# A two-layer S5/pool trunk on one core: both layers written out, the feed-forward in eight chunks, layer 1's tables made during layer 0

## The chip, the cores and the metric

One core of a Trainium2 chip runs one launch of the kernel. The metric is the device time of that launch in microseconds (us), the median over several runs. TensorE (PE) multiplies, VectorE (DVE), ScalarE (ACT) and GpSimd (POOL) do the elementwise work, and SyncE (SP) issues DMAs, as ACT and POOL also can. Each engine executes its own list of instructions in order and waits on semaphores.

## The reference

1088 frames (1024 of a prompt, 64 of a running stream) of 1024 channels pass two layers and a last RMSNorm. All of it is float32.

```python
# per layer
hn = rmsnorm(x, g_mix);  u_a, u_b = split(hn @ w_in)          # 1024 -> 512 + 512
lam_dt = lam * exp(log_dt);  lam_bar = exp(lam_dt)             # 32 groups x 64 complex states
b_bar = ((lam_bar - 1) / lam) * b
h_t = lam_bar * h_{t-1} + b_bar u_a_t                          # scan over the frames
y = Re(C h) + d * u_a;  z = gelu(y);  y_a = z * sigmoid(z @ w_glu)
y_b = (trailing means over 2/4/8/16 frames - u_b) @ w_pool * scale
x = x + concat(y_a, y_b) @ w_out
x = x + square(relu(rmsnorm(x, g_ffn) @ w_ff1)) @ w_ff2        # 1024 -> 4096 -> 1024
# returned: y of both streams, the last states, the last 15 rows of u_b, per layer
```

## The kernel before, in words

Activations lie with channels on the partitions, all 1088 frames along the free axis. A product of float32 accuracy is three fast products: each operand is split into a high part (rounded) and a low part (the rest), and high x high, low x high, high x low add up in PSUM. A **tile** is 128 output channels by 1088 frames in one of two PSUM buffers (`tile0`, `tile1`), written by 9 matmuls per 128 input channels (three products by three column chunks of 408, 408 and 272): 72 matmuls with 1024 input channels ("K=8" below), 36 with 512 ("K=4"). Weights come in **blocks** of 512 KB, one for each K=8 tile or two K=4 tiles: SP fetches block b into `w_raw` when the block two before it has been split, ACT makes `w_high` (L590), DVE makes `w_low` (L778). Two slots of each alternate.

A layer has 96 tiles. In order: 8 tiles of w_in (WIN, K=8), 4 small pool tiles (L494), 8 tiles of the w_out half for y_b ("wob", K=4), 4 of w_glu (K=4), 8 of the w_out half for y_a ("woa", K=4), and the feed-forward, 4 chunks of 1024 hidden channels, each with 8 tiles of w_ff1 (FF1, K=8) and 8 of w_ff2 (FF2, K=8).

The SSM is blocked by 8 frames (136 blocks J). Four quarters q of 8 groups each pass:

- tables from the parameters (`angles` L825, `discretised` L850, both DVE), rotations by doubling (`double` L308; groups halves on DVE and on POOL), `drive_weights(q)` L898 on DVE, `carry_weights(q)` L1198 on POOL; on PE, `prep(q)` L430 transposes the drive weights (L437) and multiplies out the intra-block kernels (L449), ACT stores those to DRAM;
- `drives(q)` on PE (L463) and ACT, then a rotation of the drives (`rotate` L290, `early_pre` L944, `pre` L939), a scan (L963) and a rotation back (`post` L974). DVE does these for some quarters, POOL does others (L1238 to L1253);
- `carry(q)` on PE (L511): intra-block and carried part into the small PSUM buffers, `output(q)` L1072 on DVE adds d*u, ACT stores the rows to DRAM (`store` L698), SP reads them back as y_a, ACT takes the GELU (L712) and splits (L714).

Since `x` shares its memory with `u_b` and the pool's buffers, x is kept in DRAM (L620, L600) and read back (L379) when the pool tiles are done; that, the carry weights (L370) and the intra-block kernels (L375) go through SP's queue in that order at block B_WOB+3. The order of work on each engine is written out by hand; the PE list interleaves the small products between WIN tiles (L469 to L485) and the carries between wob tiles (L534 to L542). Both layers are one body in a loop over l (L337, L427, L624, L807, L1178); the middle chunks of the feed-forward are loops too.

The hidden activation (`hidden` L1117): DVE takes relu times the inverse root from PSUM (L1121), squares it (L1124), splits the next weight block (L778), and makes the hidden low part (L1128); ACT makes the hidden high part (L736). FF2's tile waits before each 128 hidden channels for `hid_made` (L554 to L556) in the first tile of a chunk.

```python
def ff2(c, m, odd):
    ff_tile(odd, 16 * c + 8 + m, ghi, glo,
            None if odd else lambda k: pe.wait_ge(hid_made, l * 32 + 8 * c + k + 1))
```

RMSNorm: ACT squares x tile by tile (`finish` L592), POOL adds the squares (L1171), PE sums over the partitions (L423), ACT takes the root (L606), DVE inverts (L790).

## Time and profile before

| what | us |
| --- | --- |
| median of three runs (2304.25 to 2305.23) | 2305.21 |
| span of the profiled execution, first to last instruction | 2305.6 |
| PE busy in it | 2182.5 (95%) |
| DVE busy | 1085.5 (47%) |
| ACT busy | 422.5 (18%) |
| POOL busy | 305.1 (13%) |

The profile gives for the execution its span and the busy time in it; nothing outside the span is listed, and the span stands 0.4 us above the median of the runs. The share of an engine says little by itself here: the two feed-forwards (about 400 to 1150 us and 1520 to 2275 us) have PE busy without a break, and the stretches between them, one mixer per layer, do not. The prediction therefore reads the execution by stretches.

### The profile page before, as it was taken

What the parts mean: (1) busy time and instruction counts of PE and PEld (TensorE: products, weight loads), DVE (VectorE), ACT (ScalarE), POOL (GpSimd) and SP (SyncE); (2) the same over time, 40 slices, a digit from 0 to 9 for tenths busy, and PEclk for the clock granted to TensorE, in tenths of its full rate; (3) what the DMA queues carried; (4) which work ended last, traced back from release to release, by engine and by line L of the source; (5) the groups of instructions that cost most, each with busy time, mean ns of one, the idle gap of its engine ahead of it and who ended that gap; (6) DMA issues with size and microseconds to landing.
All of it is one profiled execution on the core that took longest, in us unless ns stands there. A gap on an engine that the chain in (4) does not pass through costs nothing.

```text
span 2305.6 us, 32257 instructions
## 1 busy us (share of the span) xinstructions
PE 2182.5 (95%) x12894; PEld 2125.5 (92%) x12894; DVE 1085.5 (47%) x1448; ACT 422.5 (18%) x462; POOL 305.1 (13%) x372
## 2 busy tenths in 40 slices
PE   6896999999999999999998979999999999999995
PEld 5785799999999999999997868999999999999995
DVE  7999445532332242233379973554224224323435
ACT  3111043210110111111221202421011101101121
POOL 4637003000000000000235630110000000000011
PEclk8998799999999999999998978999999999999998
DMA  5618221111111111111225633111111111111123
GB/s 214 135 50 170 54 71 37 46 46 45 46 45 37 45 45 45 36 45 65 95 91 113 108 112 77 37 47 46 45 37 45 45 45 40 45 42 45 45 86 125
DMA packets 72121, 153.04 MB, mean 66 GB/s; under 512 B 6752, under 2 KB 40848, under 8 KB 71776
## 3 DMA queue, kind: packets, MB, share of 16 engines
q1 hardware_dynamic: 46384, 117.79, 18.2%
q10 hardware_dynamic: 24992, 31.60, 4.3%
q0 software_dynamic: 656, 2.48, 0.3%
q8 instruction: 54, 0.88, 0.2%
q14 instruction: 35, 0.29, 0.0%
HBM read 119.96 MB, written 31.88 MB: 66 GB/s over the span
## 4 chain that ended last, share of the span: by engine, by line
PE 78%; DVE 15%; issue 5%; ACT 1%; DMA 0%; DVEq 0%; POOL 0%; ACTq 0%; SPq 0%; POOLq 0%
PE tile L405 74%; DVE drive_products L815 2%; PE small L528 1%; PE small L527 1%; DVE drive L969 1%; DVE rotations L321 1%; DVE h_low L783 1%; DVE drive L967 1%; DVE w_low L778 1%; PE small L529 1%; DVE pool_s L815 1%; DVE x L1063 1%; DVE dve_products L319 1%; DVE work_s L803 1%; DVE ub L933 1%
## 5 line engine op out<-in xcount | busy, mean ns | idle before, releaser
L405 PE MATMUL tile<-h_high,w_high 128*128 128x408 f32 (+1 forms) x1920 | 432.0, 333 | 27.8 <-DVE h_low L783 23.9
L405 PE MATMUL tile<-h_low,w_high 128*128 128x408 f32 (+1 forms) x1920 | 427.1, 331 | 0.0
L405 PE MATMUL tile<-h_high,w_low 128*128 128x408 f32 (+1 forms) x1920 | 426.8, 331 | 0.0
L1063 DVE TENSOR_TENSOR x<-tile,x 128x816 f32<-128x816 f32 (+1 forms) x192 | 129.9, 717 | 551.9 <-PE tile L405 551.9
L405 PEld LDWEIGHTS tile<-h_high,w_high 128*128 128x128 f32 x1920 | 324.3, 190 | 35.6 <-DVE h_low L783 26.6
L405 PE MATMUL tile<-hidden_high,w_high 128*128 128x408 f32 (+1 forms) x1536 | 338.4, 328 | 0.0
L405 PE MATMUL tile<-hidden_low,w_high 128*128 128x408 f32 (+1 forms) x1536 | 338.4, 328 | 0.0
L405 PE MATMUL tile<-hidden_high,w_low 128*128 128x408 f32 (+1 forms) x1536 | 338.4, 328 | 0.0
L405 PEld LDWEIGHTS tile<-h_low,w_high 128*128 128x128 f32 x1920 | 324.1, 190 | 0.2
L405 PEld LDWEIGHTS tile<-h_high,w_low 128*128 128x128 f32 x1920 | 324.0, 190 | 0.2
L590 ACT ACTIVATE w_high<-w_raw 128x1024 fp32r<-128x1024 f32 x166 | 174.4, 1051 | 784.7 <-PE tile L405 784.2
L778 DVE TENSOR_TENSOR w_low<-w_raw,w_high 128x1024 fp32r<-128x1024 f32 x166 | 217.5, 1310 | 146.0 <-ACT w_high L590 146.0
L1171 POOL TENSOR_TENSOR rms<-rms,work_s 128x1088 f32<-128x1088 f32 x20 | 54.7, 2733 | 1674.7 <-ACT work_s L597 1660.2
L1121 DVE SCALAR_TENSOR_TENSOR work_r<-tile,rms 128x816 f32<-128x816 f32 (+1 forms) x128 | 86.7, 719 | 380.4 <-PE tile L405 380.2
L405 PEld LDWEIGHTS tile<-hidden_high,w_high 128*128 128x128 f32 x1536 | 256.5, 188 | 0.0
L405 PEld LDWEIGHTS tile<-hidden_low,w_high 128*128 128x128 f32 x1536 | 256.5, 188 | 0.0
L405 PEld LDWEIGHTS tile<-hidden_high,w_low 128*128 128x128 f32 x1536 | 256.5, 188 | 0.0
L736 ACT ACTIVATE hidden_high<-work_r 128x1088 f32 (+1 forms) x64 | 71.5, 1117 | 626.8 <-DVE work_r L1121 626.8
L1124 DVE TENSOR_TENSOR work_s<-work_r 128x1088 f32<-128x1088 f32 x64 | 82.7, 1292 | 2.2
L1128 DVE TENSOR_TENSOR hidden_low<-work_s,hidden_high 128x1088 f32 (+1 forms) x64 | 82.2, 1285 | 0.0
L405 PE MATMUL tile<-y_b_high,w_high 128*128 128x408 f32 (+1 forms) x192 | 49.1, 369 | 31.7 <-DVE x L1063 31.4
L405 PEld LDWEIGHTS tile<-y_b_high,w_high 128*128 128x128 f32 x192 | 36.3, 213 | 33.9 <-DVE x L1063 32.5
(174 smaller groups left out, 1844.7 us busy)
## 6 DMA issues: line engine op xcount, KB each, us to landing
w_raw<-w_blocks SPq DMA_DIRECT2D x166, 512.0 KB, 3.5
x_kept<-x ACTq DMA_DIRECT2D x24, 544.0 KB, 2.7
x<-x_kept SPq DMA_DIRECT2D x16, 544.0 KB, 13.6
x<-x_t ACTq DMA_DIRECT2D x8, 544.0 KB, 10.4
ua_dram<-u_a SPq DMA_DIRECT2D x8, 544.0 KB, 7.4
u_blocks<-ua_dram SPq DMA_DIRECT2D x32, 136.0 KB, 6.5
ya_dram<-u_blocks ACTq DMA_DIRECT2D x64, 68.0 KB, 2.2
y_a<-ya_dram SPq DMA_DIRECT2D x8, 544.0 KB, 3.4
```

The costliest lines, as they stand in the source:

```text
L319: step(tensor_tensor(t1, w_, fi, ALU.mult))
L321: step(tensor_tensor(rot[:, ri, :, n:2 * n], t0, t1, op))
L405: last = pe.matmul(ps[tile][:, c, 0:(b - a) * J], lhs, xt[:, k, a * J:b * J], start=(k == order[0] and n == 0), stop=(k == order[-1] and n ...
L590: act.activation(whi[:, s, :], raw[:, s, :], ACT.Copy).then_inc(whi_made, 1)
L736: act.activation(out, tr[:, :], ACT.Square).then_inc(ghi_made, 1)
L778: v.tensor_tensor(wlo[:, s, :], raw[:, s, :], f32(whi[:, s, :]), ALU.subtract).then_inc(wlo_made, 1)
L815: step(v.tensor_tensor(out, a, b, op))
L1063: ins = v.tensor_tensor(xt, pt_, xt, ALU.add)
L1121: ins = v.scalar_tensor_tensor(out, pt_, 0.0, r, ALU.max, ALU.mult)
L1124: v.tensor_tensor(ts[:, :], tr[:, :], tr[:, :], ALU.mult).then_inc(sq_v, 1)
L1128: v.tensor_tensor(lo, ts[:, :], f32(hi), ALU.subtract).then_inc(hid_made, 1)
L1171: pool.tensor_tensor(rms[:, :], rms[:, :], (tr, ts)[m % 2][:, :], ALU.add).then_inc(sq_added, 1)
```

## The change

- The loop over layers and the loops in the feed-forward are gone; every instruction is written out, with the layer as a constant.
- The feed-forward has 8 chunks (NC) of 512 hidden channels: 4 tiles of w_ff1 with K=8, then 8 tiles of w_ff2 with K=4, in the order m = 0..7, k = 0..3. Weight blocks stay at 64 per layer; an FF2 block holds two tiles and is read from two blocks of the old layout.
- The tables of layer 1 (angles, discretisation, rotations, drive weights, carry weights, kernels) are made on DVE, PE and ACT inside layer 0's feed-forward: the first four pieces after the four hidden tiles of chunk 0, the quarters in chunks 1 to 4. POOL's queue stores them to DRAM, and in chunk 6 SP reads rotations and drive weights back.
- All work on the states is DVE's: rotations, carry weights, pre, scan, post. POOL keeps the sums of squares and issues DMAs. The final states are copied out of the rotated ones instead of being computed by POOL.
- d*u goes into the intra-block kernel (`fix_kernel`, DVE), and ACT instead of DVE takes the carry's result out of PSUM (`carried`).
- Layer 0's angles and discretisation are placed among the loads of x at the very start; rotations follow before the first inverse root. x of layer 0 is read back from the input, not from a kept copy.
- The carries lie elsewhere among the wob tiles, and otherwise in each layer.

```diff
+            def turned(q, sign, shift, tmp):
+                ...
+                tt(t[0], cos, re, ALU.mult)
+                tt(t[1], sin, im, ALU.mult)
+                tt(t[2], cos, im, ALU.mult)
+                tt(t[3], sin, re, ALU.mult)
+                step.wait()
+                tt(to_re, t[0], t[1], ALU.add if sign < 0 else ALU.subtract)
+                tt(to_im, t[2], t[3], ALU.subtract if sign < 0 else ALU.add)
...
 @block.sync
+                    if b == B_WOB + 2:
                         sp.wait_ge(tile_done, LT + KD)
                         sp.wait_ge(cy_out, 128 * (l + 1))
+                        sp.dma_start(cy[:, :, :, :], cy_dram[l]).then_inc(cy_in, 16)
                         sp.wait_ge(k_out, 128 * (l + 1))
...
+                            sp.dma_start(kin[CH * tau:CH * tau + CH, :, :],
+                                         k_dram[l, :, :, a:a + P]).then_inc(kin_in, 16)
                         sp.wait_ge(tile_free, LT + T_POOL + KA + 2)
+                        for m in range(6):
+                            sp.dma_start(x[:, m, :], (x_in, x_hist)[l][m]).then_inc(x_back[m], 16)
...
 @block.tensor
+                    if l == 0:
+                        if 3 <= t < 7:
+                            drives(0, t - 3)
+                        if 2 <= t < 6:
+                            turns(0, t - 2)
+                        if t >= 4:
+                            kernels(0, t - 4)
+                    elif 2 <= t < 6:
+                        drives(1, t - 2)
...
+                if l == 0:
+                    for n in range(4):
+                        wob(n)
+                    carry(0)
+                    carry(1)
+                    wob(4)
+                    carry(2)
+                    wob(5)
+                    carry(3)
+                    wob(6)
+                    wob(7)
+                else:
+                    wob(0)
+                    carry(0)
+                    wob(1)
+                    carry(1)
+                    wob(2)
+                    wob(3)
+                    carry(2)
+                    wob(4)
+                    carry(3)
+                    for n in range(5, 8):
+                        wob(n)
...
+                for cc in range(NC):
+                    for m in range(KA):
+                        ...
+                        product(n % 2, m % 2, 0, KD, hhi, hlo, ready)
+                        ...
+                        if l == 0 and m == 2 and cc in PREP_CHUNKS:
+                            turns(1, PREP_CHUNKS[cc])
+                    n = ff2_tile(l, cc, 0)
+                    for m in range(KD):
+                        ...
+                        product((n + m) % 2, m // 2 % 2, KA * (m % 2), KA, ghi, glo, None if m else
+                                lambda k: pe.wait_ge(hid_made, (l * NC + cc) * KA + k + 1))
+                        if l == 0 and m == 3 and cc in PREP_CHUNKS:
+                            kernels(1, PREP_CHUNKS[cc])
...
 @block.vector
+                if m == 1:
+                    angles(0)
+                if m == 4:
+                    discretised(0)
+            split_lo(1)
+            rotations(0, 0)
...
+                if l == 0:
+                    inverse(0)
+                    win_a(0)
+                    rotations(0, 1)
+                    rotations(0, 2)
+                    win_a(1)
+                    rotations(0, 3)
+                    drive_weights(0, 0)
+                    win_a(2)
+                    drive_weights(0, 1)
+                    carry_weights(0, 0)
+                    win_a(3)
+                    ...
+                    pooled(0, 0)
+                    v.wait_ge(lp_in, 16)
+                    for i in range(KA):
+                        y_b(i)
+                    fix_kernel(0, 3)
+                    post(0, 0)
+                    post(0, 1)
+                    wob(0)
+                    pre(0, 2, late)
+                    scan(0, 2)
+                    ...
...
+                        if l == 0:
+                            if cc == 0:
+                                (angles, discretised, lambda l: rotations(l, 0), lambda l: rotations(l, 1))[m](1)
+                            elif cc in PREP_CHUNKS:
+                                q = PREP_CHUNKS[cc]
+                                if m == 0 and q == 0:
+                                    rotations(1, 2)
+                                    rotations(1, 3)
+                                if m == 1:
+                                    drive_weights(1, q)
+                                if m == 3:
+                                    carry_weights(1, q)
...
 @block.gpsimd
+            for q in range(4):
+                carry_weights_out(0, q)
+                if q:
+                    kernels_out(0, q - 1)
+            kernels_out(0, 3)
+            states_out(0)
+            add_squares(1)
+            rotations_out()
```

PREP_CHUNKS maps the chunks 1 to 4 to the quarters 0 to 3. `drive_weights(1, 0)` waits for the store of the rotations (`rot_out`), because its products overlay them.

## Rows read from the trace of the kernel before

**Rows 1.** The page: the chain that ended last, share of the span by engine.

```profile
PE 78%; DVE 15%; issue 5%; ACT 1%; DMA 0%; DVEq 0%; POOL 0%; ACTq 0%; SPq 0%; POOLq 0%
```

**Rows 2.** Busy time by stretch: length, PE, PEld, DVE, ACT, POOL, clock, DMA, GB/s.

```profile
43.00:180.00 137.00, 124.57 (x822) 114.20 (x822) 126.20 (x243) 30.11 (x52) 61.87 (x91) 0.93 0.40 97
180.00:244.00 64.00, 43.71 (x228) 40.44 (x228) 62.77 (x120) 5.62 (x8) 36.71 (x54) 0.87 0.70 144
400.00:1150.00 750.00, 750.00 (x4501) 749.92 (x4500) 256.21 (x263) 114.09 (x110) 15.29 (x6) 1.00 0.15 49
1166.00:1301.00 135.00, 122.89 (x824) 113.28 (x823) 125.09 (x240) 29.59 (x51) 60.52 (x83) 0.94 0.37 86
1301.00:1366.00 65.00, 47.52 (x234) 43.49 (x234) 63.60 (x121) 6.12 (x9) 37.52 (x57) 0.82 0.67 151
```

**Rows 3.** The chain in order of time: start, length, what.

```profile
305.41 1.36 DVE x L1063 x2
...
400.90 753.00 PE tile L405 x4518
...
1154.97 13.77 PE tile L405 x81
...
1426.59 1.35 DVE x L1063 x2
```

**Rows 4.** Timeline of DVE and ACT around one FF1-to-FF2 step: start, length, instruction.

```profile
481.95 1.36 DVE L1121 SCALAR_TENSOR_TENSOR work_r<-tile,rms 128x816 f32<-128x816 f32 x2 [6.09 <-PE tile L405]
...
486.58 1.28 DVE L1128 TENSOR_TENSOR hidden_low<-work_s,hidden_high 128x1088 fp32r<-128x1088 f32 x1
```

**Rows 5.** Timeline of PE: prep(0) up to the next tile, and prep(1) after its wait.

```profile
82.82 1.03 PE L437 MATMUL small<-prep_in,x_quarter 128*128 128x128 f32 x8
87.86 0.77 PE L405 MATMUL tile<-h_high,w_high 128*128 128x408 f32 x3
...
113.12 0.58 PE L449 MATMUL small<-y_quarter,bbar_re 64*16 64x128 f32 x2 [9.10 <-POOL y_quarter L1216]
```

**Rows 6.** Timeline of DVE: drive weights, a doubling, a rotation, with and without POOL beside.

```profile
86.27 0.68 DVE L815 TENSOR_TENSOR drive_products<-power_re,bbar_re 128x512 f32<-128x512 f32 x1
...
90.38 0.24 DVE L1027 COPY rotations<-phasor 128x4 f32<-128x4 f32 x2
...
91.64 0.17 DVE L318 TENSOR_TENSOR drive_products<-rotations 128x8 f32<-128x8 f32 x1
...
194.20 1.40 DVE L321 TENSOR_TENSOR rotations<-dve_products 128x128 f32<-128x128 f32 x1
...
210.00 0.71 DVE L299 TENSOR_TENSOR dve_products<-rotations,drive 128x544 f32<-128x544 f32 x1
...
214.19 1.35 DVE L1063 TENSOR_TENSOR x<-tile,x 128x816 f32<-128x816 f32 x2
```

**Rows 7.** The DMA queue of SP around the end of WIN in layer 0: start, length of issue.

```profile
176.56 0.33 SPq L370 DMA_DIRECT2D carry_weights<-cy_dram  x1
177.00 16.88 SPq L375 DMA_DIRECT2D intra_weights<-k_dram  x8
194.15 8.33 SPq L379 DMA_DIRECT2D x<-x_kept  x8
```

**Rows 8.** Busy time in stretches of 4 us, columns as in rows 2.

```profile
188.00:192.00 4.00, 3.73 (x22) 3.73 (x23) 3.90 (x9) 1.27 (x2) 3.52 (x6) 1.00 1.28 95
208.00:212.00 4.00, 1.86 (x6) 1.82 (x7) 3.97 (x7) 0.00 (x0) 0.84 (x4) 0.50 1.02 410
248.00:252.00 4.00, 4.00 (x13) 3.00 (x14) 0.71 (x3) 0.00 (x0) 1.18 (x4) 0.50 0.03 10
280.00:284.00 4.00, 4.00 (x24) 3.03 (x23) 1.24 (x4) 0.00 (x0) 0.00 (x0) 1.00 0.00 0
```

**Rows 9.** DMA issues on the page: size of each, median us from issue to landing.

```profile
k_dram<-k_stage ACTq DMA_DIRECT2D x16, 32.0 KB, 1.6
...
k_dram<-zeros POOLq DMA_DIRECT2D x1, 224.0 KB, 8.1
```

More of the change, by code:

```diff
@@ L394, in _, with products @@
         @block.tensor
         def _(pe):
-            def product(tile, slot, half, n_k, xh, xl, ready=None, order=range(KD)):
-                order = order[:n_k]
+            def products(tile, slot, col, k, xh, xl, first, last):
+                for n, (wt, xt) in enumerate(((whi, xh), (whi, xl), (wlo, xh))):
+                    lhs = wt[:, slot, col * P:(col + 1) * P]
+                    for c, (a, b) in enumerate(CHUNKS):
+                        mm = pe.matmul(ps[tile][:, c, 0:(b - a) * J], lhs, xt[:, k, a * J:b * J],
+                                       start=(first and n == 0), stop=(last and n == 2))
+                return mm
@@ L399, in product @@
+            def product(tile, slot, col0, n_k, xh, xl, ready=None, backwards=False):
+                order = list(range(n_k))[::-1] if backwards else list(range(n_k))
                 for k in order:
@@ new lines, in kernels @@
+            def kernels(l, q):
+                d = prep_of[l]
+                pe.wait_ge(y_quart, l * 4 + q + 1)
+                for gl in range(2):
+                    out = small_at(SM["kernel", l, q, gl])
+                    rows = slice(ST * gl, ST * gl + ST)
+                    for g in range(4):
+                        for ri, b in enumerate((d.bbr, d.bbi)):
+                            mm = pe.matmul(out[0:CH, g * P:(g + 1) * P], b[rows, 4 * q + g, :],
+                                           d.yq[rows, ri, g, 0:BLK, :].rearrange("p t c -> p (t c)"),
+                                           start=(ri == 0), stop=(ri == 1))
+                    mm.then_inc(small_done, 1)
@@ new lines, in drives @@
+            def drives(l, q):
+                pe.wait_ge(ublk_in[q], 16 * BLK * (l + 1))
+                if l == 0:
+                    pe.wait_ge(small_free, SM["turn", 0, q, 1] + 1 + 2)
+                elif q == 0:
+                    pe.wait_ge(bt_in, 16)
+                for g in range(4):
+                    n = SM["drive", l, 4 * q + g]
+                    out = small_at(n)
+                    bt = stage0[:, g] if l == 0 else bt_all[:, 4 * q + g]
+                    for gl in range(2):
+                        for ri in range(2):
+                            mm = pe.matmul(out[ST * gl:ST * gl + ST, ri * J:(ri + 1) * J],
+                                           bt[:, ri, ST * gl:ST * gl + ST],
+                                           ublk[:, 2 * (4 * q + g) + gl, :], start=True, stop=True)
+                    mm.then_inc(small_done, 1)
@@ L469, in _ @@
+            pe.wait_ge(ones_set, 1)
+            for l in range(LAYERS):
+                LB, LT = l * NB, l * NT
                 for t in range(KD):
@@ L607, in roots, with turns @@
                                    scale=1.0 / DM, bias=eps_col[:, :]).then_inc(small_free, 1)
+            def turns(l, q):
+                d = prep_of[l]
+                if l == 0 and q:
+                    act.wait_ge(small_done, SM["drive", 0, 4 * q - 1] + 1)
+                if l:
+                    if q == 0:
+                        act.wait_ge(rot_out, 16)
+                    else:
+                        act.wait_ge(bt_out, 16 * q)
+                for ri in range(2):
+                    n = SM["turn", l, q, ri]
+                    act.wait_ge(small_done, n + 1)
+                    act.activation(d.bt[:, :, ri, :], sm[n % 2][:, :].rearrange("p (g n) -> p g n", n=P),
+                                   ACT.Copy).then_inc(small_free, 1)
@@ new lines, in kernels @@
+            def kernels(l, q):
+                d = prep_of[l]
+                if l * 4 + q:
+                    act.wait_ge(k_out, 32 * (l * 4 + q))
+                if l == 0 and q == 0:
+                    act.wait_ge(ua_out, 16 * KA)
+                for gl in range(2):
+                    n = SM["kernel", l, q, gl]
+                    act.wait_ge(small_done, n + 1)
+                    act.activation(d.kst[:, gl, :, :], sm[n % 2][0:CH, :].rearrange("p (g n) -> p g n", n=P),
+                                   ACT.Copy).then_inc(small_free, 1)
```

1484 lines of the change are left out of this document (753 added, 731 removed).

## The prediction

> **What bounds the kernel now.** I read the page's chain first: 78% PE, 15% DVE [rows 1]. As a share this only says that PE is nearly the bound everywhere, so I went on to the busy time by stretch [rows 2]. In 400 to 1150 us PE is busy 750.00 of 750.00 at clock 1.00: the feed-forward is purely PE's, one matmul each 753.00/4518 = 0.1667 us [rows 3], so a K=8 tile (72) takes 12.0 us and a K=4 tile (36) 6.0. DVE is busy a third of it, so there is room beside PE, and nothing to win for PE. In the mixers it is the other way round. From 43 to 180 DVE is busy 126.20 of 137, from 180 to 244 62.77 of 64 while PE has 43.71; layer 1 repeats this (125.09 of 135, 63.60 of 65) [rows 2]. PE's idle time and its low clock there are what can be won. Layer 1's WIN starts at 1154.97 and the last wob tile is added at 1426.59, so this mixer takes 271.6 us [rows 3].
>
> I take the change in four stretches and measure each against the profiled execution (span 2305.6; the runs' median is 0.4 below, so the sum is made on 2305 without correction).
>
> **Feed-forward, both layers: +14 each.** The matmul count is the same. What changes is when FF2's first tile needs the last hidden part. After an FF1 tile, DVE starts at 481.95 and finishes the low part at 486.58 + 1.28 = 487.86, 5.9 us later [rows 4]. Before, that part was k=7 of a K=8 tile, needed 7 x 1.5 = 10.5 us into it: hidden. Now it is k=3 of a K=4 tile, needed 4.5 us in. With 0.2 us for the end of the last matmul and 0.1 for the wait, PE stands 5.9 + 0.3 - 4.5 = 1.7 us, in each of 16 chunks: 27 us, half of it per layer. Nothing covers it, as the k and m orders are plain and the two PSUM tiles leave PE nothing else in its list. Bounds: 1.4 (no overheads) to 2.5 a chunk, 22 to 40. The doubled number of adds to x (1.35 us each [rows 6]) is hidden: DVE has 6 us a tile. The weight reads keep a cadence of 12 us a block.
>
> **Tables in layer 0's feed-forward: +35.** PE's part: transposes and kernels of a quarter took 82.82 to 87.86 with one wait of 0.85 in between, so 4.2 us [rows 5]; four make +17, on the path because PE has no gap there. DVE's part is hidden where a piece fits behind a hidden tile (12 - 5.9 = 6.1 us): drive weights take 90.38 - 86.27 = 4.1, carry weights (576 for 512 elements) 4.6 [rows 6]. It doesn't fit in two places. A doubling of few elements costs about 1.0 us (copies and first one 90.38 to 91.64), one of 512 about 4.1; in between I scale: rotations piece 0 (8 doublings, 240 elements in all) 9.5 us, piece 1 (4, 768) 8.7, pieces 2 and 3 4.4 each [rows 6]. Chunk 0: DVE is already late by the inverse root; angles (3.5) and discretised (6) use the slack up, and piece 0 stands ahead of the last hidden part. Walking DVE's list gives 9 us of wait in FF2's first tile instead of 1.7, then 2 more because piece 1 stands ahead of the first add: +10. After a wait of 9.10 before, the kernels of prep(1) ran slow [rows 5]; a wait of this length costs about 4 more in low clock. Chunk 1: pieces 2 and 3 (8.8), then the 2.2 MB store of the rotations, must be done before drive weights 0, which PE's transposes wait for in order. At the 410 GB/s of one row the store takes 5.4 us, at 95 GB/s 23 [rows 8]; its rows are 17 KB long, so I take 7.5 with issue, and get +4 (bounds 0 to 20). Together 17 + 14 + 4 = +35 (17 to 55). The read back in chunk 6 (4.3 MB, 11 us at 410 GB/s) fits into the 19 us that a block is fetched ahead.
>
> **Layer 1's mixer: -52.** Without tables, DVE has in it 7 (inverse) + 9.6 (four u_a) + 4 x 4.2 (pre) + 4 x 3.7 (scan) + 4 x 5 (post) + 12 (u_b) + 21 (pool sums) + 6 (y_b) + 14 (wob) = 121 us (where no group shows a duration of this kind, it is read from the same timeline of DVE as rows 6), and PE becomes the bound. PE's walk from WIN's start: tiles 96 and three sums 2, drives after four of them 11, so WIN ends at 109; pool tiles and their ACT-DVE relay to 122; wob 0 at 128. Then the new wait: the carries now stand right behind wob 0, and they need the intra-block kernels. These are read after WIN, in SP's queue behind the carry weights. Before, the issue ran from 176.56 to 193.9 and then x [rows 7], with 95 GB/s at 1.28 of the DMA engines' share at 188 and 410 GB/s from 208 on, when x came [rows 8]: the kernels land some 28 us after the end of WIN. Before, five wob tiles stood ahead and hid this. Now 109 + 28 = 137, so PE waits 9 us, and carry 0 may run at the low clock. A carry (4 of 16 pairs) takes 8.7 us at clock 1.00 and twice the matmul time at 0.50: 24 matmuls in 4 us against 13 [rows 8]. With it slow (16), wob 1 partly slow (8), three carries 26 and six wob tiles 36: 137 + 16 + 8 + 26 + 36 = 223 against 271.6, -49; with all at full speed 208, -64. I take -52.
>
> **Layer 0's head and mixer: +9.** Added to DVE: angles and discretised stand in the head, where DVE was already busy throughout: 9.3 us later (they leave the mixer). Then rotations in pieces, 27 us, all on DVE; carry weights 4 x 4.6 = 18 come from POOL, as do half the pre and post. Taken off: the lock between the two. Beside POOL's products a DVE product of 128 elements took 1.40 us, while one of 544 took 0.71 when alone [rows 6]; POOL's 61.87 and 36.71 us [rows 2] go. With clean durations DVE's list from the split of block 1 (52 us) to the last post sums to 178 us, before waits: 230. The waits, by walking the four lists: PE's first transposes wait for drive weights 0 until 95 us, and the WIN tile behind them is late for u_a (5); carry weights 2 for a small product (3); y_b for ACT, which holds each kernel until the store before it has landed, 4 us through POOL's queue, between 1.6 and 8.1 [rows 9] (9); and the largest, the first wob add waits for x. The last kernel is fixed only behind y_b, at 204, is stored by 208, the kernels' read takes 20 more and x comes after it: 231 us against 214 when DVE is there (17). So DVE's last post ends near 264, where PE has passed wob 3 at 248. From there carries 35 and four wob tiles 24 make 307 at full clock, 323 with two carries and a wob tile slow as before, against 305.41 [rows 3]: +1 to +18, with an error of my walk of about 10 either way. I take +9.
>
> A rule that speaks against the change: the last kernel's store goes through POOL's queue now, and the rows there are 8.1 us for the one store by POOL on the page against 1.6 for the same matrix from ACT [rows 9]; I take 4. By the Trainium skill (SBUF — State Buffer, "SBUF: two separate sides") a DMA issued on GpSimd has its descriptors written by that engine, which a two-port VectorE operation locks out, 620 ns alone against about 3100 beside a copy. By it this store would come about 2.5 us later than alone, and layer 0's mixer would be longer by as much; no row here shows it.
>
> The loops' turns cost nothing now: 0.1667 us a matmul hold across all of them [rows 3]. The Trainium skill (Runtime: NRT & Kernel Launch, "Instruction fetch mechanics") has a taken branch out of the sequential window stall the fetch, so that unrolling would gain; by that rule the sum would be lower, by the rows it is not.
>
> **Sum.** 14 + 14 + 35 - 52 + 9 = +20, so 2305 + 20 = 2325 us.
>
> **Rivals.** (A) My forecast: 2325, own range 2308 to 2342. Chance 0.50. (B) Faster: DVE relieved of POOL walks ahead of PE in layer 0 as well, and the clock stays up through the carries since ACT drains PSUM at once. Then layer 0's mixer gains 12, layer 1's 64, and the feed-forward costs 27 + 28 = 55: -21, 2284. For it: DVE stands at 98% from 180 to 244 in both layers beside a busy POOL [rows 2], and a full-clock carry is seen at 280. Against it: the same carries ran at 0.50 at 248 [rows 8], and the x wait of layer 0 is a matter of order. It decides from the point where layer 0's first wob add comes before 220 us. Chance 0.28. (C) The chunk stalls are worse: waits of 9 us in chunks 0 and 1 leave PE at the low clock, the rotations' store takes the long bound, and layer 0's x comes late: 27 + 55 - 45 + 15 = +52, 2357. For it: the store shares queues with the weights. Against it: the feed-forward's DMA share is 0.15 [rows 2]. Chance 0.14. (D) The gains and costs cancel: 2305, chance 0.08, the middle between A and B.
>
> **How the numbers follow.** About 0.2% (5 us) is what a measurement tells from no change. Faster by more: B and a little of A's and D's edge, 0.30. Within: 0.08. Slower: 0.62. The range that leaves out 2 in 10 goes from 2282 (just below B) to 2350 (most of A, the near half of C).
>
> **What would show it.** The time between FF1's last tile and the fourth k of FF2 in the profile after: a wait of PE on hidden_low of 1.5 to 2 us, sixteen times. PE busy in the feed-forward of layer 0 below full, with one wait near 9 us in its first chunk. Layer 1 from WIN's start to the last wob add near 220 us, with PE waiting for a DMA before its first carry. Layer 0's last wob add between 300 and 325 us, and DVE waiting some 15 us for x. The prediction is wrong if the feed-forwards run without gaps, since then the sum is -7, or if layer 1's mixer stays above 240.

## The result: 0.3% slower, 2310.6 us where 2325 was forecast

| | median of the runs | profiled run | its span |
|---|---|---|---|
| before | 2305.14 us (20 runs) | about 2307 | 2305.6 |
| after | 2310.55 us (20 runs, 2305.72 to 2319.65) | 2317.74 | 2315.9 |

The ratio is 1.0033, 95% interval 1.0022 to 1.0044. The direction was right, the move was +5.4 us and not +20. The time of the kernel before's profiled run isn't on record; in all of its runs that have both, the time is 1.5 to 1.6 us above the span, hence about 2307. So this execution was some 2 us slower than its kernel's median, and that of the changed kernel 7.2.

The stretches first, in the profiled executions. The marks are those of [rows 3]: PE's start of layer 1's WIN and the start of each layer's last wob add. WIN starts before the last part of x is complete: the last FF2 add ends 0.3 us after that mark in the kernel before and 6.1 after it in the changed one.

| stretch | forecast | before | after | difference |
|---|---|---|---|---|
| start to layer 0's last wob add | +9 | 305.4 | 314.4 | +9.0 |
| to layer 1's WIN | +49 | 849.6 | 887.2 | +37.6 |
| to layer 1's last wob add | -52 | 271.6 | 225.9 | -45.7 |
| to the end | +14 | 879.0 | 888.4 | +9.4 |
| sum | +20 | | | +10.3 |

Busy time of the changed kernel by stretch, columns as in [rows 2]:

```profile
43.00:180.00 137.00, 117.56 (x776) 109.39 (x776) 123.24 (x252) 23.60 (x41) 15.09 (x15) 0.92 0.28 83
180.00:244.00 64.00, 41.84 (x199) 36.47 (x198) 34.16 (x88) 8.20 (x12) 2.06 (x4) 0.73 0.64 130
400.00:1150.00 750.00, 728.26 (x4427) 719.38 (x4426) 342.08 (x483) 109.78 (x117) 14.32 (x22) 0.99 0.17 57
1155.00:1290.00 135.00, 130.41 (x847) 125.93 (x846) 88.99 (x142) 36.51 (x47) 17.83 (x7) 1.00 0.34 109
1290.00:1355.00 65.00, 52.60 (x259) 45.77 (x258) 44.89 (x107) 8.58 (x13) 0.00 (x0) 0.84 0.71 141
```

In layer 1's first mixer stretch DVE falls from 125 busy us to 89: the tables are gone from it. The feed-forward, full before, now leaves PE idle for 21.7 of 750 us. In layer 0 DVE is busy only 34 of 64 us from 180 on. Four of PE's waits (total, times, longest) say for what; the largest total, for `h_low`, was 23.9 us before. The 13.6 us more all stand ahead of 50 us, in the head where the angles and the discretisation went, for the 9.3 that were forecast there:

```profile
PE tile L427 <- DVE h_low L865: 37.5, 9, 12.0
PE tile L427 <- DVE hidden_low L1324: 31.5, 16, 8.5
PE tile L427 <- DVE x L1200: 18.3, 2, 18.1
PE small L463 <- DVE x_quarter L1012: 12.1, 2, 9.7
PE small L566 <- issue: 8.7, 1, 8.7
```

The last four in time order, from the timelines of DVE and PE (the bracket is the idle time ahead):

```profile
234.06 1.35 DVE L1200 TENSOR_TENSOR x<-tile,x 128x816 f32<-128x816 f32 x2 [17.96 <-DMA x<-x_t]
...
456.01 1.28 PE L427 MATMUL tile<-hidden_high,w_high 128*128 128x408 f32 x3 [8.46 <-DVE hidden_low L1324]
...
539.82 1.09 PE L463 MATMUL small<-prep_in,x_quarter 128*128 128x128 f32 x8 [2.38 <-DVE x_quarter L1012]
...
1342.16 0.79 PE L566 MATMUL small<-u_blocks,intra_weights 128*128 128x136 f32 x2 [8.74 <-issue]
```

They are the waits of the forecast, near its sizes: 17, 9, 4 and 9 us had been walked out. The chain through layer 1's feed-forward shows the small one, one turn per chunk of 97.16 us:

```profile
1558.97 1.29 DVE L1319 TENSOR_TENSOR work_s<-work_r 128x1088 f32<-128x1088 f32 x1
1562.21 1.28 DVE L1324 TENSOR_TENSOR hidden_low<-work_s,hidden_high 128x1088 fp32r<-128x1088 f32 x1
...
1563.55 91.18 PE tile L427 x549
```

After 1563.55 the next restart is at 1660.71. Of the 31.5 us that PE waits for `hidden_low` the first chunk has 8.46, so it stands 1.53 us in each of the other 15. The row also has what I had not expected: 91.18 / 549 = 0.1661 us a matmul, where it was 753.00 / 4518 = 0.1667 [rows 3].

### The profile page after: what moved, and what is told of

Its sections match the earlier page's. It is cut to its first block and busy times, and to the rows that moved or that the text cites. A ratio compares the mean times of both kernels' runs of the same rounds, so it can differ in the third digit from the quotient of the medians.

```text
span 2315.9 us, 29009 instructions
## 1 busy us (share of the span) xinstructions
PE 2160.1 (93%) x12894; PEld 2098.9 (91%) x12894; DVE 1120.3 (48%) x1622; ACT 423.4 (18%) x483; POOL 120.4 (5%) x80
## 3 DMA queue, kind: packets, MB, share of 16 engines
q10 hardware_dynamic: 12960, 17.96, 2.5%
## 5 line engine op out<-in xcount | busy, mean ns | idle before, releaser
L1200 DVE TENSOR_TENSOR x<-tile,x 128x816 f32<-128x816 f32 x320 | 216.6, 718 | 580.6 <-PE tile L427 552.8
L427 PE MATMUL tile<-hidden_high,w_high 128*128 128x408 f32 (+1 forms) x1536 | 340.6, 330 | 31.6 <-DVE hidden_low L1324 31.5
L860 DVE TENSOR_TENSOR w_low<-w_raw,w_high 128x1024 fp32r<-128x1024 f32 x164 | 210.4, 1283 | 101.3 <-ACT w_high L635 101.3
L815 ACT ACTIVATE hidden_high<-work_r 128x1088 fp32r<-128x1088 f32 x64 | 71.4, 1116 | 645.7 <-DVE work_r L1316 645.7
L1324 DVE TENSOR_TENSOR hidden_low<-work_s,hidden_high 128x1088 fp32r<-128x1088 f32 x64 | 82.2, 1284 | 0.0
L865 DVE SCALAR_TENSOR_TENSOR h_low<-x,layer_params,h_high 128x1088 fp32r<-128x1088 f32 x24 | 43.9, 1830 | 27.3 <-ACT h_high L650 27.3
## 6 DMA issues: line engine op xcount, KB each, us to landing
x<-x_t SPq DMA_DIRECT2D x8, 544.0 KB, 13.3
x<-x_kept SPq DMA_DIRECT2D x8, 544.0 KB, 13.3
```

Source lines behind the costliest of these rows:

```text
L427: mm = pe.matmul(ps[tile][:, c, 0:(b - a) * J], lhs, xt[:, k, a * J:b * J], start=(first and n == 0), stop=(last and n == 2))
L815: act.activation(ghi[:, m, :], tr[:, :], ACT.Square).then_inc(ghi_made, 1)
L860: v.tensor_tensor(wlo[:, b % 2, :], raw[:, b % 2, :], f32(whi[:, b % 2, :]), ALU.subtract).then_inc(wlo_made, 1)
L865: v.scalar_tensor_tensor(hlo[:, m, :], x[:, m, :], gain[:, m:m + 1], f32(hhi[:, m, :]), ALU.mult, ALU.subtract).then_inc(h_made, 1)
L1200: ins = v.tensor_tensor(xt, pt_, xt, ALU.add)
L1324: v.tensor_tensor(glo[:, m, :], ts[:, :], f32(ghi[:, m, :]), ALU.subtract).then_inc(hid_made, 1)
```

## The experiments

All were timed in turns with the kernel before; medians in us. The ratios come from the comparison with its runs in turn and are not the quotients of two medians. The stretches in the table are of the profiled executions: to the end of layer 0's last wob add; from the end of the last WOA add to that of the last FF2 add (FF 0, FF 1); and between FF 0 and layer 1's last wob add (mixer 1).

| kernel | median | ratio, 95% | mixer 0 | FF 0 | mixer 1 | FF 1 |
|---|---|---|---|---|---|---|
| before | 2305.1 | | 306.8 | 767.3 | 272.6 | 767.3 |
| after | 2310.6 | 1.0033 | 315.8 | 810.2 | 221.1 | 776.6 |
| e1_order | 2295.6 | 0.9948 (0.9934, 0.9962) | 312.4 | 806.9 | 221.0 | 764.4 |
| e2_place | 2302.5 | 0.9995 (0.9982, 1.0008) | 310.9 | 801.2 | 220.3 | 776.4 |
| e3_xfirst | 2312.9 | 1.0034 (1.0022, 1.0046) | 314.3 | 809.9 | 220.9 | 776.4 |
| e4_l1wob | 2306.2 | 1.0012 (0.9998, 1.0025) | 315.5 | 812.0 | 219.3 | 776.5 |
| e5_petables | 2298.6 | 0.9966 (0.9953, 0.9979) | 313.7 | 796.9 | 220.1 | 776.5 |
| e7_spaced | 2299.0 | 0.9981 (0.9960, 1.0003) | 312.1 | 810.4 | 211.5 | 776.5 |
| b1_unroll | 2305.5 | 0.9993 (0.9982, 1.0005) | 307.3 | 767.3 | 272.2 | 767.3 |
| b2_layers | 2295.0 | 0.9952 (0.9926, 0.9978) | 306.4 | 767.2 | 272.8 | 767.2 |
| b3_shift | 2339.7 | 1.0136 (1.0090, 1.0182) | 328.9 | 762.3 | 298.1 | 763.9 |
| c1_all | 2272.9 | 0.9849 (0.9834, 0.9864) | 314.9 | 792.2 | 220.3 | 764.4 |
| c2_spaced | 2261.3 | 0.9828 (0.9793, 0.9862) | 304.4 | 794.0 | 204.6 | 764.4 |

A profiled execution is one of its kernel's runs. Most lie within 3 us of the median, but those of the changed kernel (7.2 us above), e4 (11.3, the slowest of 11), c1 (10.5, the slowest of 5) and b2 (10.2) do not, and b3's lies 6.2 above. Mixer 0 is the same work in the changed kernel, e1, e2, e4, e5 and e7, and reads 310.9 to 315.8 us: less than 5 us there is no effect.

**e1_order: is the wait per chunk a matter of FF2's order?**

```diff
-                    for m in range(KD):
+                    for m, ks in ((0, (0, 1, 2)), (1, (0, 1, 2)), (0, (3,)), (1, (3,))):
+                        ...
+                    for m in range(2, KD):
```

> The changed kernel with FF2's first two tiles of every chunk interleaved on PE: tile 0 with k = 0 to 2, tile 1 with k = 0 to 2, then tile 0's k = 3 and tile 1's k = 3; all else as in the changed kernel. My theory (the wait of 1.53 us on the last hidden part is a matter of how much of FF2 stands ahead of it, 4.5 us against the 5.9 that ACT and DVE need): with 9 us of matmuls ahead of it the wait goes in all 15 plain chunks, 15 x 1.5 = 23 us, and that of 8.5 us in the first chunk shrinks by 4.5; layer 1's and layer 0's mixers are unchanged: 23 to 27 us below the changed kernel's 2310.6, about 2285. Rival 1 (FF2 becomes bound by what comes later, since tile 0 ends later, both tiles end within 1.5 us of each other and the adds of tile 0 and 1 then lag, so that FF2's third tile waits for a free PSUM tile): half of it or nothing comes back, 2298 to 2310, with a wait of PE on tile_free's side in place of the one on hidden_low. Rival 2 (PE's wait is recorded time in which the engine would have paid a weight load or a fetch anyway): 2310.

Layer 1's feed-forward went from 776.6 to 764.4: 12.2 us, 8 x 1.53, and the waits are gone. So the cause of this term is shown. Layer 0's gave only 3.3 more. Five of its chunks gained 1.5 each. The first became 2.4 us longer (107.9 for 105.5), for PE waits there twice, first for DVE's drain of the fourth hidden tile and then for the late adds. The second gained nothing: behind the wait for the drive weights the clock was at 0.50 from 538.0 to 541.4. The last became 1.6 us longer, for PE waits for the adds there too (third row), and 1.15 us more ahead of WIN:

```profile
446.74 1.27 PE L427 MATMUL tile<-hidden_high,w_high 128*128 128x408 f32 x3 [3.91 <-DVE work_r L1326]
460.95 1.25 PE L427 MATMUL tile<-hidden_high,w_high 128*128 128x408 f32 x3 [3.82 <-DVE x L1210]
...
1180.13 0.73 PE L427 MATMUL tile<-hidden_high,w_high 128*128 128x408 f32 x3 [1.25 <-DVE x L1210]
```

The first chunk, where DVE has rotations in its list, shows rival 1. In all it gained 15 us for the 23 to 27 expected.

**e2_place: is the first chunk's wait DVE's rotations?**

```diff
-                (angles, discretised, lambda l: rotations(l, 0), lambda l: rotations(l, 1))[m](1)
+                if m < 2:
+                    (angles, discretised)[m](1)
...
+        if l == 0 and cc == 0 and m < 7:
+            ...
+            for n2, h2 in (((1, 0), (1, 1)), ((2, 0), (2, 1)), ...)[m]:
+                doubled(1, n2, h2)
```

> The changed kernel with pieces 0 and 1 of layer 1's rotations moved: they no longer stand behind hidden tiles 2 and 3 of the first chunk, but, two doublings at a time, behind the adds of FF2 tiles 0 to 6 of that chunk. My theory (the wait of 8.5 us in the first chunk is VectorE's list, with 9.5 us of rotations ahead of the last hidden part, and the low clock behind it follows from the wait): the wait falls to the 1.5 us of the other chunks, and the clock stays at 1.00: 7 us from the wait and 2 to 3 from the clock, about 10 us below the changed kernel, 2300. Rival 1 (the doublings behind the adds make the adds late, and FF2's tiles then wait for a free PSUM tile): 1 to 2 us come back at each of 3 or 4 tiles, 2305. Rival 2 (the wait comes from the inverse root and the hidden tiles themselves, not from the tables): unchanged, 2310.

```profile
442.81 0.77 PE L427 MATMUL tile<-hidden_high,w_high 128*128 128x408 f32 x3 [1.53 <-DVE hidden_low L1324]
```

The first chunk takes 96.4 us for 105.5, the median is 8.1 us lower, and the three matmuls behind the wait take 0.77 us, not 1.28: at the end of the long wait the clock had been at 0.50. So 6.9 us of the 9.1 are the wait and the rest is clock. My theory held, and no wait for a free PSUM tile took the place of the old one.

**e5_petables: what do the tables cost PE?**

```diff
-                    for g in range(4):
+                    for g in range(4 if l == 0 else 1):
```

> The changed kernel with PE's share of layer 1's tables cut to a quarter: of each quarter's 8 transposes 2 and of its 16 small products 4 are done, the rest is left out (so that three quarters of layer 1's kernels and drive weights aren't computed); the waits and all of VectorE's and ScalarE's work stay. My theory (the tables' matmuls are added to PE's list, 4.2 us a quarter at full clock, 17 in all, because PE has no gap in the feed-forward): 3/4 of 17 less, 13 us, and layer 0's feed-forward 797 us instead of 810; the kernel 2298. Rival (these small matmuls cost next to nothing, and what the tables cost PE is the waiting for VectorE, which stays): within 3 us of the changed kernel, 2308 to 2311.

Layer 0's feed-forward was 13.3 us shorter. In the changed kernel a chunk with tables takes 101.40 us and one without 97.16, so a quarter costs 4.24; with a quarter of the matmuls 98.13. That is linear in PE's work, and 4 x 4.24 = 17.0 stands beside the forecast's 17.

**e3_xfirst: is the 18 us wait for x a matter of SP's queue?**

```diff
+                    if l == 0 and b == B_WOB + 2:
+                        sp.wait_ge(tile_free, LT + T_POOL + KA + 2)
+                        for m in range(6):
+                            sp.dma_start(x[:, m, :], x_in[m]).then_inc(x_back[m], 16)
```

> The changed kernel where, in layer 0 alone, SyncE issues the reads of x tiles 0 to 5 ahead of those of the carry weights and of the kernels, and not behind them. My theory (the 18 us that VectorE and PE stand before layer 0's first wob add are the order of SyncE's queue: x waits behind the kernels' read, which waits for the last kernel's store): the wait goes, but PE then meets the carries, which need the kernels that now come some 4 us later, after seven wob tiles: layer 0's last wob add comes 8 to 16 us earlier, 2297 to 2302. Rival 1 (the kernels are what everything waits for, and the 18 us reappear in front of the first carry): less than 3 us, 2308 to 2311. Rival 2 (the reads of x, started early, collide with the drive weights' and kernels' stores and make WIN's last tiles late): slower than 2311.

The first wob add came at 210.6 instead of 234.1, and then PE met the kernels:

```profile
212.10 0.73 PE L432 MATMUL tile<-y_b_high,w_high 128*128 128x408 f32 x3 [1.20 <-DVE x L1205]
220.95 0.76 PE L432 MATMUL tile<-y_b_high,w_high 128*128 128x408 f32 x3 [2.65 <-DVE x L1205]
238.31 0.79 PE L571 MATMUL small<-u_blocks,intra_weights 128*128 128x136 f32 x2 [9.59 <-issue]
```

The wait was one of 18 and is now three of 13.4 together, the largest ahead of the first carry, as rival 1 has it. Mixer 0 is 1.5 us shorter, which is within its spread, and the ratio is 1.0034 for 1.0033: nothing gained, the clock having been at 0.50 from 232.6 to 273.6. The median of 2312.9 is in rival 2's range, but its reason is not what happened: wob 0 began at 198.8, not later than in the changed kernel (203.6). This pointed at the carries.

**e4_l1wob and e7_spaced: the wait before the carries, or the carries?** In layer 1 of the changed kernel no two carries stand side by side, and PE waits 8.7 us before carry 0. e4 swaps carry 0 and wob 1: the wait is filled, but carries 0 and 1 now stand side by side. e7 fills the wait too and keeps the carries apart. Its edit:

```diff
                     wob(0)
-                    carry(0)
-                    wob(1)
-                    carry(1)
-                    wob(2)
-                    wob(3)
-                    carry(2)
-                    wob(4)
-                    carry(3)
+                    for q in range(4):
+                        wob(q + 1)
+                        carry(q)
```

> The changed kernel with PE's order in layer 1's mixer changed from wob 0, carry 0, wob 1, carry 1 to wob 0, wob 1, carry 0, carry 1; all else as in the changed kernel. My theory (PE stands 8.7 us before carry 0 because the intra-block kernels land late, and carry 0 then runs at half clock for what it waited): a wob tile of 6 us fills the wait, which falls to 2 to 3 us; 6 us less from the wait, and up to 8 more if the clock then stays at 1.00: layer 1's mixer 207 to 215 us instead of 221, the kernel 2297 to 2305. Rival (the carries' results are what the end of the mixer waits for, through VectorE's y_b or ScalarE's copies, so that the later carries only move the wait behind them): 2308 to 2311, with a longer wait of PE on z_low or on x.

> The changed kernel with PE's order in layer 1's mixer changed to wob 0, 1, carry 0, wob 2, carry 1, wob 3, carry 2, wob 4, carry 3, wob 5 to 7: no two carries stand side by side. With wob 1 ahead of carry 0 the wait of 8.7 us had shrunk to 1.7, and yet the clock fell to 0.50, 3 us into the carries and with PE busy 4.00 us of 4.00, and stayed there for 30.8 us: that mixer gained 1.8 us, not 6 to 14. Theory 1 (the carries themselves draw the low clock: matmuls of 136 columns with a weight load each; a row of two carries gives it, a wob tile between any two prevents it or ends it soon): low clock in the carries' stretch 14 us or less instead of 31 (24 in the changed kernel), layer 1's mixer 208 to 213 us instead of 221, the kernel 2298 to 2303. Theory 2 (the low clock comes from what stood before, the waits for y_b and the short pool matmuls, and is only granted late): low clock 24 to 31 us again, mixer 219 to 221, 2306 to 2310.

First the changed kernel itself, 4 us at a time (columns as in [rows 2]):

```profile
1338.00:1342.00 4.00, 0.00 (x0) 0.00 (x0) 0.00 (x0) 0.00 (x0) 0.00 (x0) 0.50 1.13 181
1342.00:1346.00 4.00, 3.84 (x12) 2.90 (x12) 2.40 (x4) 0.00 (x0) 0.00 (x0) 0.50 1.03 416
...
1358.00:1362.00 4.00, 4.00 (x16) 3.93 (x17) 0.00 (x0) 0.26 (x1) 0.00 (x0) 0.60 0.57 97
1362.00:1366.00 4.00, 4.00 (x26) 3.86 (x25) 0.37 (x1) 0.44 (x1) 0.00 (x0) 1.00 0.25 42
```

The clock falls to 0.50 in the wait, at 1337.3, and is back at 1361.2, in the wob tile behind carry 0.

In e4 PE waits 1.7 us for the kernels and not 8.7, yet the mixer gains 1.8 us in the profiled execution. PE's busy time in it (length, busy, clock, DMA share, GB/s):

```profile
1338.00:1342.00 4.00, 4.00 (x26) 1.00 1.30 109
1342.00:1346.00 4.00, 2.28 (x14) 1.00 0.97 350
1346.00:1350.00 4.00, 4.00 (x17) 0.60 1.02 408
1350.00:1354.00 4.00, 4.00 (x14) 0.50 0.48 195
...
1370.00:1374.00 4.00, 4.00 (x13) 0.50 0.59 180
1374.00:1378.00 4.00, 4.00 (x16) 0.56 0.99 341
1378.00:1382.00 4.00, 4.00 (x26) 1.00 0.17 35
```

Ahead of the carries PE was full and the clock at 1.00. Two carries stand side by side from 1344, PE stays busy, and the clock is at 0.50 for 30.8 us. In e7 the same view:

```profile
1336.00:1340.00 4.00, 3.88 (x20) 0.89 1.04 415
1340.00:1344.00 4.00, 4.00 (x14) 0.50 0.91 368
1344.00:1348.00 4.00, 4.00 (x14) 0.50 0.05 17
1348.00:1352.00 4.00, 4.00 (x14) 0.50 0.25 43
1352.00:1356.00 4.00, 4.00 (x24) 0.91 0.54 97
```

One carry and part of the tile behind it still run at 0.50, 13.6 us, and the later three don't. Mixer 1 takes 211.5 us, for 219.3 in e4 and 221.1 in the changed kernel.

Two things are to be read apart. From the changed kernel to e7 the carries are apart in both. The mixer gains 9.6 us, 7.2 of them the shorter wait (8.74 to 1.56) and the other 2.4 the clock, so the wait does count, as the forecast had it. From e4 to e7 the wait is the same (1.7 and 1.6) and the order differs: 30.8 us at 0.50 against 13.6. So a long wait isn't needed for the low clock: in e4 it comes 2.8 us into the carries (matmuls of 136 columns, the products with the states over 64 rows), with PE busy without a break, and it lasts as long as they follow each other. What part the short wait ahead has in its start isn't separated. By medians e7 is 11.6 us below the changed kernel, at its theory's 2298 to 2303, and the intervals are apart. e4 is 4.3 below it, between its theory and its rival. Against e4, e7 has 7.2 us by medians with intervals that touch, and the 30.8 us are those of e4's slowest run, so the size of that difference is not settled.

**b1_unroll, b2_layers, b3_shift: why is a matmul 0.0006 us shorter?** b1 and b2 write the loops out; b3 keeps them and moves the buffers: the weight tiles, the work tiles and the constants by 128 bytes, as in the changed kernel, and `d_and_init` elsewhere.

```diff
-            with pe.Fori(0, LAYERS) as l:
+            for l in range(LAYERS):
```

```diff
-        R = G + 2 * H
+        R = G + 2 * H + 32
-        dd = at("d_and_init", S + 216, [P, ND])
+        dd = at("d_and_init", H + 12608, [P, ND])
```

> The kernel before with one edit: the loops of the feed-forward (over chunks and tiles, on PE, ScalarE, VectorE and SyncE) are written out; the loop over the layers stays, and so do the order of all work, the four chunks of 1024 and everything in the mixers. In the changed kernel's trace a feed-forward matmul takes 91.18 / 549 = 0.1661 us, in that of before 753.00 / 4518 = 0.1667. Theory (the loops cost it: registers, jumps, fetching): the trace shows 0.1661 here too, and the time is 0.35% of the 1580 us of both feed-forwards below before, 5.5 to 7 us, about 2298 against 2305. Rival 1 (the two profiled executions stood on chips or in moments with a clock that differs by 0.35%, and the loops cost nothing): same time as before within 0.1%, and the pitch follows the chip: before's own executions on that chip show the same. Rival 2 (the written-out code must be fetched, 0.7 MB more of instructions, and that costs): slower than before by over 2 us.

> The kernel before with every loop written out on every engine, the one over the layers too; order, chunks, buffers and waits as before. With only the feed-forward's loops written out, three matmuls (408, 408 and 272 columns) still began every 0.500 us, as in before; in the changed kernel and its variants they begin in turn every 0.501 and 0.492 us, 0.4% less, some 6 to 7 us over both feed-forwards. Theory 1 (it is the written-out program as a whole, registers or code in the loop over the layers): 0.4965 on the mean here, feed-forwards of 764.3 instead of 767.3 us, and with what the mixers' matmuls gain 7 to 8 us below the kernel before, 2297 to 2298. Theory 2 (it is where the buffers lie: the changed kernel's weight tiles stand 128 bytes further on, and its hidden tiles elsewhere): 0.500 and 767.3 here, and 2305.

> The kernel before, loops and all, with the raw, high and low weight tiles, the work tiles and the constants 128 bytes further on in SBUF, where the changed kernel has them; to make room the states' start values lie elsewhere and are read at the end of WIN. Written-out loops left the beat of three matmuls (408, 408 and 272 columns) at 0.500 us, and in the changed kernel it is 0.4965. Theory (the beat depends on where the weights or what they meet in a transfer lie): 0.4965 here, both feed-forwards 764.3 us instead of 767.3, and 7 us below before, 2298. Rival (it is neither code nor these addresses, but the chunks of 512 and their smaller hidden tiles): 0.500, 767.3 us, and 2303 to 2306.

Matmuls of PE begun in the 500 us from 1700 on: b1, b2 and b3, one row of each kernel's windows (length, busy, clock, DMA share, GB/s).

```profile
1700.00:2200.00 500.00, 500.00 (x3002) 1.00 0.13 45
```

```profile
1700.00:2200.00 500.00, 500.00 (x3002) 1.00 0.15 46
```

```profile
1700.00:2200.00 500.00, 500.00 (x3023) 1.00 0.14 44
```

Written-out loops change nothing, the move of the buffers does: the row of 4518 matmuls reads 753.02 us in b1 and this in b3.

```profile
1567.41 747.99 PE tile L407 x4518
```

So b1 speaks for its rival 1 in part (no gain from the loops), b3 for its theory: 762.3 and 763.9 us for the 764.3 expected. The chip, the other part of that rival, is out: b1, e1, e2 and e3 were timed on one chip, and b1 has the old pitch there and the other three the new one. b3's time missed its 2298 by 42 us. Both its mixers are 22 and 25 us longer; its edit also holds SP at the end of WIN until all WIN tiles are done, which is the likely reason and wasn't tested by itself. Which of the moved buffers matters, and why the beat of three alternates between 0.501 and 0.492 us in the changed kernel, stays open.

b2 has a gain of 0.5% that is in no feed-forward: its nine runs lie near 2280.7, 2294 and 2305 us with a mean granted clock of 0.973, 0.968 and 0.965, and the profiled one is of the last kind. The kernel before does the same more rarely: 5 of the 20 runs of the result lie at 2294 to 2297. In its later runs, whose clocks are on record, three at 2294 to 2297 have 0.971, one at 2286.6 has 0.974 and the others 0.962 to 0.968. So b2's gain may be no more than more of its nine runs in the lower steps. The steps of some 11 us go with the clock; in which stretch they arise was not profiled.

**c1_all and c2_spaced: together.** c1 holds e1, e2, e3 and e4, with wob 0 to 5 ahead of the four carries in layer 0. c2 is c1 with e7's order in layer 1 and this one in layer 0, where carries 1 and 2 still stand side by side:

```diff
-                    for n in range(6):
-                        wob(n)
-                    for q in range(4):
-                        carry(q)
+                    for n in range(5):
+                        wob(n)
+                    carry(0)
+                    wob(5)
+                    carry(1)
+                    carry(2)
                     wob(6)
+                    carry(3)
                     wob(7)
```

> The changed kernel with four edits together: FF2's first two tiles interleaved in every chunk; pieces 0 and 1 of layer 1's rotations behind the adds of the first chunk's FF2 tiles; in layer 0 the reads of x tiles 0 to 5 ahead of the tables' reads, with PE's order wob 0 to 5, the four carries, wob 6, wob 7; in layer 1 wob 0, wob 1, carry 0. My theory (each removes its own wait, and they do not share one): 12 us in each feed-forward, 9 in the first chunk, 6 to 12 in layer 0's mixer, 6 to 12 in layer 1's: 2310.6 less 45 to 57, 2254 to 2266. Rival 1 (the interleaving and the moved rotations meet in the first chunk, where VectorE is late whatever the order: with the interleaving alone PE waited 19.9 us there for an add to x): the first chunk gives back nothing, 2265 to 2275. Rival 2 (the carries at the end of layer 0's mixer leave GLU waiting for z): 5 to 8 us back, 2262 to 2272.

> The kernel with the four edits together, with other orders of PE in the mixers: layer 0 wob 0 to 4, carry 0, wob 5, carry 1, carry 2, wob 6, carry 3, wob 7 (there: wob 0 to 5, the four carries, wob 6, wob 7), layer 1 wob 0, 1, carry 0, wob 2, carry 1, wob 3, carry 2, wob 4, carry 3, wob 5 to 7. In that kernel the clock was 0.50 for 44 us in layer 0 (its four carries and the wob tile behind them) and for 34 in layer 1, so half of each was lost. Theory 1 (rows of carries draw the low clock): 20 to 30 us less of low clock in the two mixers together, 10 to 15 us less time than its 2272.9: 2258 to 2263. Theory 2 (the carries run at the low clock wherever they stand): 2270 to 2275; with carry 3 one wob tile nearer to the end, GLU may wait for z up to 4 us more.

c1 came to 2272.9: the first chunk did give back its 10 us (94.9 for 105.5), both feed-forwards have theirs, and the mixers gave nothing in the profiled execution. Rival 1's time was right, its reason wrong (the 19.9 us that it names stood in layer 0's mixer, at the first wob add; in the first chunk PE waited 3.9 and 3.8). The clock again, c1 from 200 and from 1300, then c2 from 200 and from 1290:

```profile
200.00:320.00 120.00, 111.59 (x508) 0.78 0.55 128
...
1300.00:1400.00 100.00, 98.16 (x467) 0.81 0.60 129
```

```profile
200.00:320.00 120.00, 109.17 (x549) 0.87 0.56 133
...
1290.00:1390.00 100.00, 92.83 (x516) 0.97 0.62 141
```

In layer 0 of c1 the four carries run in a row from 246.1 to 298.9, and the clock is at 0.50 from 259.7 to 304.1:

```profile
250.00:254.00 4.00, 4.00 (x24) 1.00 0.48 139
258.00:262.00 4.00, 3.35 (x14) 0.72 0.61 144
...
298.00:302.00 4.00, 4.00 (x14) 0.50 0.37 64
```

With the carries further apart mixer 0 is 10.5 us and mixer 1 15.7 us shorter in the profiled executions, but c1's is 10.5 us above its median. By medians the whole step is 11.7 us, in the 10 to 15 expected; each has five runs, and the intervals overlap (0.9834 to 0.9864 and 0.9793 to 0.9862), so its size is open. The mean clock speaks for it over all runs: 0.975 to 0.978 in c2, 0.965 to 0.977 in c1. At 2261.3, ratio 0.9828, c2 is 1.7% faster than the kernel before, clear of noise, and faster than the changed kernel.

## Why the prediction was half right

- **FF2 in halves (+14 a layer).** Right in mechanism and nearly in size: 1.53 us a plain chunk for 1.7, so 12.2 a layer (FF 1: -12.2 when undone by e1). The overheads of 0.3 us on the last matmul were too much by half; 1.53 less the 1.4 of the bare walk leaves 0.13.
- **Tables in layer 0's feed-forward (+35).** PE's part 17.0 for 17 (e5). Chunk 1: 2.38 for 4, so the store of the rotations wasn't late (issued at 528.5, landed 7.2 us later, for 7.5). The first chunk was mis-sized: +14 forecast, +9.1 measured (e2). The wait is as walked (8.46), the second stall of 2 us did not come, and the low clock cost 2.2 and not 4.
- **Layer 1's mixer (-52).** -45.7. The walk came out: PE's wait of 9 us for the kernels was 8.74, carry 0 took 15.6 us for 16 (wob 1 begins at 1357.75, the row below) and the slow wob 1 7.8 for 8. The walk had given -49, and -64 with all at full speed, and I took -52; that is half of the miss. The other half is the start of carry 0, 140.6 us after WIN's start for 137. The reason for the low clock was right in part: it falls in the wait, but without one it comes as well (e4, e7).

```profile
1357.75 1.27 PE L427 MATMUL tile<-y_b_high,w_high 128*128 128x408 f32 x3
```

- **Layer 0's head and mixer (+9).** +9.0, and the wait for x 17.96 for 17. That it hits to 0.1 is luck: the same mixer in e1, e2, e4, e5 and e7 has this mark at 309.5 to 314.2, 4 to 9 above the kernel before, and the walk's own error was given as 10. And "a matter of order" was wrong as a promise: with x early the time did not fall (e3); mixer 0 was shorter only in c2, where the carries' order changed as well. The last kernel's store by POOL's queue landed 1.9 us after its issue, near ACT's 1.6 [rows 9], not the 4 that I took; the three pairs before it took 2.8 to 4.0. By the Trainium skill (SBUF — State Buffer, "SBUF: two separate sides") a copy on VectorE beside such a store makes it longer. Beside this one, issued at 207.4, VectorE ran products (207.01 to 209.62) and no copy, and the row counts from the issue, so no run here tests that rule.
- **Matmuls cost the same (0).** The step that failed outright: the forecast kept 0.1667 us a matmul, and the trace has 0.1661; by b3 (0.1656) it is a matter of where the buffers lie; by b1 and b2 the loops have no part in it. Layer 1's feed-forward shows it, 9.3 us longer where the waits alone are 12.2: -3 us a layer, -6 in all. Nothing in the profile before gave it away. The loops themselves were rightly priced at nothing: b1 and b2 leave the feed-forward at 767.2 to 767.3 us. The Trainium skill (Runtime: NRT & Kernel Launch, "Instruction fetch mechanics") has a taken branch out of the fetched window stall the fetch; no such stall shows here.
- **The sum.** It failed by three terms that were too dear and one that was left at nothing. Between the profiled executions the forecast was +20 and the traces give +10.3: 6 from the shorter matmuls, 5 from the first chunk, 1.6 from chunk 1, 3.6 from the stalls' size, less 6.3 in layer 1's mixer, which makes 9.9 for the 9.7 between them. Another 5 us is the change from profile to median: the profiled run of the changed kernel stands 7.2 above its median, with a clock of 0.968 where others of its 20 have up to 0.974, that of the kernel before some 2. The forecast set the span of the kernel before, 0.4 above its median, beside run times and so saw nearly none of this; the changed kernel's part it could not see.
- **Rival B** (carries at full clock) had the wrong condition, the first wob add before 220 us. In e3 that add came at 210.6 and nothing was gained, and carries at full clock came with other orders of carries and wob tiles (e7, c2).

## What to carry to other kernels

Halving the depth of a tile halves the cover for the part that arrives last: compare the time to that part with the drain's latency (4.5 against 5.9 us here), and if it falls short, interleave two tiles. A wait that is taken away counts only if the clock behind it holds, so read the granted clock in 4 us rows across the work that comes next: in e4's profiled run short matmuls side by side took back in clock most of what the wait had cost. Where a forecast is a few parts in a thousand, the spread of single executions is as large as the terms, and the profiled one must be placed among the runs on both sides.

## What the runs showed of the hardware

- With four carries side by side PE's clock stayed at 0.50 while PE was busy 4.00 of 4.00 us (c1: from 259.7 to 304.1, into the wob tile behind them). With a wob tile between any two, it came back in the first tile behind the first carry (e7) or never fell during the carries (layer 1 of c2: 0.97 on the mean from 1290 to 1390).
- The same 4518 matmuls took 753.02 us or 747.99 us, with the weight and work tiles and the constants 128 bytes further on in SBUF and one small tile elsewhere (b1, b3).
- Executions of one unchanged program on one chip (b2) differed in steps of about 11 us, with the mean clock: 2280.7, 2294 and 2305 us at 0.973, 0.968 and 0.965.
